# A two-block transformer kernel on one core: state copies on ScalarE, states advanced one direction per level, the output gate's product a chunk earlier, output projection from level 0 of the last chunk

## The reference, cut to what matters

```python
pc = hc @ w_in[:, :COL_Q]                       # 256 context tokens: keys, values, decays
s_f = gla_final_state(kc, vc, gfc)              # the states that the recurrence starts from
s_b = gla_final_state(flip(kc), flip(vc), flip(gbc))

def step(s, inp):                               # gla_chunked: a chunk of tokens
    b = jnp.cumsum(gc, axis=1)
    o_inter = einsum('bihk,bhkv->bihv', qc * exp(b), s)
    att = einsum('bihk,bjhk,bijhk->bijh', qc, kc, exp(b_i - b_j) masked)
    o_intra = einsum('bijh,bjhv->bihv', att, vc)
    s_new = s * exp(b_last) + einsum('bjhk,bjhv->bhkv', kc * exp(b_last - b), vc)

o_gla = rmsnorm(o_f + o_b, g_head) * silu(og)   # og: 512 columns of x @ w_in
o_sc = sb * dwconv_row(sc * sx, w_sc, b_sc)     # sb, sc, sx: columns of x @ w_in
yx = concatenate([o_gla, o_sc])
x = x + gt1 * rmsnorm(yx @ w_out, g_post_mix)
```

## Time and profile before

| | us |
|---|---|
| median of three runs | 1448.08 (1447.05 to 1450.49) |
| the profiled execution | 1445.49 |
| its span, first to last instruction | 1443.7 |
| around the span | 1.8 |
| granted TensorE clock, mean | 0.978 |

### The profile page before, as it was taken

The page is one execution under the profiler, slowest core; times in us unless marked ns, Lnnn a source line. Parts: engine busy times, 40 slices in busy tenths (PEclk is TensorE's granted clock), DMA queues, the critical chain, the costliest instruction groups (busy, mean ns, idle before and its releaser), DMA issues.

```text
span 1443.7 us, 19719 instructions
## 1 busy us (share of the span) xinstructions
PE 1378.6 (95%) x6923; PEld 1113.7 (77%) x6923; DVE 895.8 (62%) x1274; ACT 397.4 (28%) x757; POOL 836.0 (58%) x651
## 2 busy tenths in 40 slices
PE   6899899998799999999999999999899999999998
PEld 4678678877488888887877888676688888888887
DVE  4687687753766666673028699646766888886000
ACT  3442223322422222201013202355413333332000
POOL 1343434426566666677756677532367777777775
PEclk8999999989799999999989999999999999999999
DMA  9457222112033333354332333221133333333332
GB/s 355 150 186 221 57 57 60 59 45 84 16 94 98 102 89 100 98 156 140 102 88 73 89 88 88 73 59 44 42 91 88 102 93 96 102 89 94 92 94 84
DMA packets 224459, 142.05 MB, mean 98 GB/s; under 512 B 5611, under 2 KB 211088, under 8 KB 224400
## 3 DMA queue, kind: packets, MB, share of 16 engines
q1 hardware_dynamic: 221333, 136.45, 31.6%
q10 hardware_dynamic: 3067, 4.78, 1.0%
HBM read 139.12 MB, written 2.10 MB: 98 GB/s over the span
## 4 chain that ended last, share of the span: by engine, by line
PE 83%; DVE 9%; issue 3%; POOL 2%; ACT 2%; DMA 0%; POOLq 0%; SPq 0%; DVEq 0%; ACTq 0%
PE ps L555 25%; PE ps L557 24%; PE ps L556 24%; PE ps L853 2%; DVE norm_acc L1713 1%; POOL w_lo L518 1%; DVE ada_acc L1810 1%; PE ps L1096 1%; PE ps L1125 1%; PE ps L1112 1%; DVE SS L2015 1%; ACT h_hi L1210 1%; DVE xT L2186 1%; POOL w_hi L515 1%; DVE h_lo L1734 1%
## 5 line engine op out<-in xcount | busy, mean ns | idle before, releaser
L518 POOL TENSOR_TENSOR w_lo<-raw,w_hi 128x1024 fp32r<-128x1024 f32 x213 | 535.5, 2514 | 17.8
L555 PE MATMUL ps<-h_hi,w_hi 128*128 128x512 f32 x1064 | 426.2, 401 | 13.2 <-DVE h_lo L1734 8.3
L557 PE MATMUL ps<-h_hi,w_lo 128*128 128x512 f32 x1064 | 417.5, 392 | 0.0
L556 PE MATMUL ps<-h_lo,w_hi 128*128 128x512 f32 x1064 | 417.4, 392 | 0.0
L514 POOL TENSOR_TENSOR w_hi<-raw,cst 128x16 fp32r<-128x16 f32 x213 | 62.3, 292 | 560.3 <-PE ps L557 503.7
L555 PEld LDWEIGHTS ps<-h_hi,w_hi 128*128 128x128 f32 x1064 | 201.5, 189 | 66.4 <-issue 18.3
L557 PEld LDWEIGHTS ps<-h_hi,w_lo 128*128 128x128 f32 x1064 | 201.5, 189 | 43.6
L556 PEld LDWEIGHTS ps<-h_lo,w_hi 128*128 128x128 f32 x1064 | 202.0, 190 | 39.6
L515 POOL TENSOR_SCALAR w_hi<-raw 128x1008 fp32r<-128x1008 f32 x213 | 232.4, 1091 | 0.0
L2104 DVE SCALAR_TENSOR_TENSOR f_acc<-ps,par,f_acc 128x441 f32<-128x441 f32 (+2 forms) x176 | 122.3, 695 | 50.2 <-ACT f_acc L1210 27.9
L555 PE MATMUL ps<-f_hi,w_hi 128*128 128x512 f32 x352 | 138.3, 393 | 0.6 <-POOL w_lo L518 0.6
(11 more groups left out here) (301 smaller groups left out, 1958.0 us busy)
## 6 DMA issues: line engine op xcount, KB each, us to landing
raw<-in_w_up SPq DMA_DIRECT2D x88, 512.0 KB, 3.7
raw<-in_w_in SPq DMA_DIRECT2D x59, 512.0 KB, 3.7
raw<-in_w_down SPq DMA_DIRECT2D x32, 512.0 KB, 3.7
ada_first<-in_w_ada SPq DMA_DIRECT2D x8, 1024.0 KB, 10.2
raw<-in_w_out SPq DMA_DIRECT2D x16, 512.0 KB, 3.5
v_tok<-in_w_ada SPq DMA_DIRECT2D x14, 512.0 KB, 5.3
raw<-in_w_down SPq DMA_DIRECT2D x16, 384.0 KB, 3.3
ada<-in_w_ada SPq DMA_DIRECT2D x10, 512.0 KB, 4.9
```

What stands on the lines that cost most here:

```text
L518: pool.tensor_tensor(w_lo[:, slot % 2, :], raw[:, slot, :], w_hi[:, slot % 2, :].bitcast(F32), ALU.subtract).then_inc(S("lo_split"), 1)
L555: nc.tensor.matmul(dst, lhs_hi, rhs_hi, start=first, stop=False)
L556: nc.tensor.matmul(dst, lhs_hi, rhs_lo, start=False, stop=False)
L557: return nc.tensor.matmul(dst, lhs_lo, rhs_hi, start=False, stop=last)
```

## The change

Five edits, all in the mixer of the first block.

1. `keep_state` moves from VectorE to ScalarE. ScalarE's row n of the key loop is now `key_decay(n)`, `keep_state(n-1)`, the copy of the turned keys n. The exp of `dec` into `small` (what the states are multiplied with) is made at n = 2, not at n = 5.
2. The states advance one direction at a time, 4 instructions each: `forward(0)` to `forward(2)` in the key loop (n = 3 to 5), `backward(0)` ahead of chunk 0, `forward(3)` in level 1, `backward(1)` to `backward(3)` in levels 2 to 4.
3. The output gate: the tanh of og moves from level 0 of its own chunk to level 4 of the chunk before (`branch_tanh`), its product from level 0 to level 5 of the chunk before (`branch_gate`); for chunk 0 they stand in the key loop and ahead of chunk 0. Bank 0 is thus free a chunk earlier, and the semaphores of the branch are counted anew.
4. `out_s` is given out by the table `MIX_EARLY`: in levels 0, 1 and 2 of chunk 3 the first three k of tiles 0, 1, 2 (9 matmuls each), in level 3 their last k (9), in levels 4 and 5 half of tile 3 each (6), in level 6 tile 4 (12). The last k needs the branch half of chunk 3 (`ys`), which is made in level 2. `MIX_BANKS` is reordered, so that a tile's bank is one that is free by then.
5. `head_gate` is made chunk by chunk, in levels 2, 4 and 5 of chunk 3.

```diff
-    MIX_BANKS = [0, 1, 2, 3, 7, 4, 5, 6]
+    MIX_BANKS = [0, 2, 3, 1, 7, 4, 5, 6]
...
+        MIX_EARLY = [[(0, 0, 3)], [(1, 0, 3)], [(2, 0, 3)], [(0, 3, 4), (1, 3, 4), (2, 3, 4)], [(3, 0, 2)], [(3, 2, 4)], [(4, 0, 4)]]
+        def mix_early(n):
+            free = {0: ("gated_og", CHUNKS), 1: ("branch_act", 2 * CHUNKS), 2: ("branch_dve", 2 * CHUNKS - 1), 3: ("branch_dve", 2 * CHUNKS)}
+            for m, k0, k1 in MIX_EARLY[n]:
+                if k0 == 0 and m in free:
+                    pe.wait_ge(S(free[m][0]), free[m][1])
+                out_tile("out_s", m, ys_hi, ys_lo, 0, range(k0, k1))
...
-                elif n >= 2:
-                    if n == 2:
-                        pe.wait_ge(S("branch_act"), 2 * CHUNKS)
-                        pe.wait_ge(S("branch_dve"), 3 * CHUNKS)
-                    out_tile("out_s", n - 2, ys_hi, ys_lo, 0)
+                else:
+                    mix_early(n)
...
+        def keep_state(n, c):
+            act.wait_ge(S("state_mm"), n + 1)
...
+            for dst, src in todo:
+                ins = activate(dst, src, ACT.Copy)
+            ins.then_inc(S("state_read"), 1)
...
+            if n >= 1:
+                keep_state(n - 1, STATE_ORDER[n - 1])
             act.wait_ge(S("ke_turned"), n + 1)
...
             activate((g_qe, g_att)[n % 2][:, :], ps[:, 4 + 3 * (n % 2), :], ACT.Copy).then_inc(S("ket_copied"), 1)
+            if n == 3:
+                branch_tanh(0)
...
+        act.wait_ge(S("ket_copied"), ALL_CHUNKS)
         exp_level(0)
+        keep_state(ALL_CHUNKS - 1, STATE_ORDER[-1])
...
+                elif n == 4 and c < CHUNKS - 1:
+                    branch_tanh(c + 1)
...
+        def forward(n):
+            dve.wait_ge(S("decay_ready"), 1)
+            dve.wait_ge(S("state_read"), n + 2)
...
-            if n >= 1:
-                keep_state(n - 1, STATE_ORDER[n - 1])
-        keep_state(ALL_CHUNKS - 1, STATE_ORDER[-1])
+            if n >= 3:
+                forward(n - 3)
...
         offset(0)
         offset(1)
+        branch_gate(0)
+        backward(0)
+        dve.wait_ge(S("ke_turned"), ALL_CHUNKS)
         decayed(0)
...
-                if c == 0 and 2 <= n < 2 + CHUNKS:
-                    if n > 2:
-                        dve.wait_ge(S("states_done"), n - 2)
-                    advance_states(n - 2)
-                if n == 5 and c == CHUNKS - 1:
-                    head_gate(False)
+                if c == 0 and n == 1:
+                    forward(CHUNKS - 1)
+                elif c == 0 and 2 <= n < 1 + CHUNKS:
+                    backward(n - 1)
+                if n == 5 and c < CHUNKS - 1:
+                    branch_gate(c + 1)
+                if c == CHUNKS - 1 and n in (2, 4, 5):
+                    head_gate((0, 1, 2)[(2, 4, 5).index(n)])
```

More of the change, by code:

```diff
@@ L797, in branch @@
                 if tile >= 1:
-                    pe.wait_ge(S("branch_act" if n == 2 else "branch_dve"), (3 * tile, 3 * tile, 2 * tile, 3 * tile - 2)[n] - (n == 0))
+                    done = (("gated_og", tile), ("branch_dve", 2 * tile), ("branch_act", 2 * tile), ("branch_dve", 2 * tile - 1))[n]
+                    pe.wait_ge(S(done[0]), done[1])
                 elif n == 0:
@@ L887, in head_spread, with out_tile @@
             mm.then_inc(S("o_spread"), 1)
-        def out_tile(name, m, hi, lo, ready):
+        def out_tile(name, m, hi, lo, ready, ks=range(4)):
             u = FIRST[name] + m // 2
             first = name == "out_s"
-            if m % 2 == 0:
+            if m % 2 == 0 and ks[0] == 0:
                 wait_unit(u)
-            for k in range(4):
+            for k in ks:
                 if m == 0:
@@ L901, in out_tile @@
                             hi[:, k, :], lo[:, k, :], first and k == 0, not first and k == 3)
+            if ks[-1] < 3:
+                return
             if m % 2:
@@ L1349, in _, with branch_tanh @@
         act.wait_ge(S("gate_done"), 2)
+        def branch_tanh(i):
+            act.wait_ge(S("units_done"), FIRST["branch"] + 4 * i + 1)
+            activate(og[:, i, :], ps[:, 0, :], ACT.Tanh, scale=0.5).then_inc(S("branch_act"), 1)
         def key_decay(n):
@@ L1395, in branch_in @@
         def branch_in(i):
[L1397 to L1400, removed]
+            act.wait_ge(S("units_done"), FIRST["branch"] + 4 * i + 3)
             if i >= 1:
-                act.wait_ge(S("branch_dve"), 3 * i)
+                act.wait_ge(S("branch_dve"), 2 * i)
             if i >= 2:
@@ L1407, in branch_center @@
         def branch_center(i):
-            act.wait_ge(S("branch_dve"), 3 * i + 1)
+            act.wait_ge(S("branch_dve"), 2 * i + 1)
             if i >= 1:
@@ L1873, in ke, with advance, backward @@
             ins.then_inc(S("ke_ready"), 1)
[L1875 to L1883, removed]
+        def advance(rows, dst, src, c):
+            for h in range(GH):
+                cols = slice(h * P, (h + 1) * P)
+                ins = vec.scalar_tensor_tensor(dst[rows, cols], src[rows, cols],
+                                               small[rows, h * ALL_CHUNKS + c:h * ALL_CHUNKS + c + 1],
+                                               dst[rows, cols], ALU.mult, ALU.add)
+            return ins
+        def forward(n):
+            dve.wait_ge(S("decay_ready"), 1)
+            dve.wait_ge(S("state_read"), n + 2)
+            if n:
+                dve.wait_ge(S("forward_done"), n)
+            src, c = (SS[:, n - 1, :], n - 1) if n else (s_tmp, CHUNKS + 1)
+            advance(slice(0, DK), SS[:, n, :], src, c).then_inc(S("forward_done"), 1)
+        def backward(n):
+            m = CHUNKS - 1 - n
+            dve.wait_ge(S("state_read"), ALL_CHUNKS if n else 2)
+            if n:
+                dve.wait_ge(S("backward_done"), n)
+            src, c = (SS[:, m + 1, :], m + 1) if n else (s_tmp, CHUNKS)
+            advance(slice(DK, P), SS[:, m, :], src, c).then_inc(S("backward_done"), 1)
         for n in range(10, EARLY_KEYS):
@@ L1996, in head_scale, with head_gate @@
                 .then_inc(S("head_scaled"), 1)
[L1998 to L2002 removed]
+        def head_gate(c):
+            tok = slice(c * P, (c + 1) * P)
+            dve.wait_ge(S("head_scaled"), c + 1)
+            dve.wait_ge(S("gated_og"), CHUNKS)
             vec.tensor_tensor(oT[:, :, tok], oT[:, :, tok], og[:, :, tok], ALU.mult).then_inc(S("head_gated"), 1)
[L2005 removed]
+        dve.wait_ge(S("ke_ready"), ALL_CHUNKS)
         offset(0)
         offset(1)
+        branch_gate(0)
+        backward(0)
+        dve.wait_ge(S("ke_turned"), ALL_CHUNKS)
         decayed(0)
[L2009 to L2025 removed]
         dve.wait_ge(S("masks_loaded"), 16)
@@ L2056, in _ @@
         head_scale(CHUNKS - 1)
-        head_gate(True)
+        head_gate(CHUNKS - 1)
         for h in range(GH):
```

37 lines of the change are left out of this document (12 added, 25 removed).

## The result

In the comparison made for the prediction the changed kernel took 1440.16 us (median, 1437.6 to 1442.81, 6 runs) and the kernel before 1448.6 us (1445.69 to 1450.49, 6 runs): ratio 0.9947, 95% interval 0.993 to 0.9963. The profiled execution of the changed kernel took 1442.81 us (span 1441.0). A second comparison, with more runs, gave 1441.9 us (10 runs) against 1445.75 (28 runs): ratio 0.9967, interval 0.9953 to 0.998. The two intervals have only gains of some 5 to 7 us in common. The forecast was 1439; its sum was 9.3 us. The trace shows that one of the two terms of this sum was right and the other wasn't.

What follows compares the result with a forecast made beforehand. PE was busy 95% of the span, so only its waits and lower clock could be won. 3.5 us (chunk 0 with key loop) plus 5.8 (chunk 3) made 9.3 off 1448.08: 1439 us, range 1433.5 to 1444.

Steps and rivals of the forecast that it cites:

- Chunk 3: Last chunk: early out tiles bring `outputs` at 313.5 us against 319.36, 5.8 us gained, bounds 3.4 and 9.1.
- rival B: PE is fed nearly throughout: 7 of 8.3 us in chunk 0, 8 of 9.1 in chunk 3; 1434, chance 0.15.
- Key loop: Chain from a states product to the next turn of keys, with ScalarE's copies: 0.6 us lost, bounds 0 and 1.4.
- ScalarE's copies "back to back": In the key loop, copies of 0.594 us each were taken 0.5 apart, making a turn's chain 3.5 us.
- Chunk 0: VectorE sets the pace; 4.6 us less state work, 1.0 taken back by GpSimd hold-ups, bounds -1.5 and +3.5.
- rival A: VectorE keeps the pace: 1.0 gained in chunk 0 with key loop, 3.4 to 4 in chunk 3; 1443, chance 0.2.
- The clock: PE's clock sank after idles of 2.3 and 1.6 us; idles up to 1.1 in the key loop left it 1.00.
- PE still isn't the limit: In chunk 0, PE's own levels would end at 200 us, against 203.4 for VectorE after the change.
- Behind the mixer: Tail after chunk 3's output: every distance stays that of before.
- C: Key loop: PE idles some 2 us a turn, the clock falls to 1.2 GHz; 4 slower, 1452, chance 0.04.
- D: Early tiles or chunk 1's branch wait for unit or bank as before; 0 to 2 us gained, 1447, chance 0.06.
- signs of being wrong: Key loop over 1.5 us longer, states above 0.5, chunk 3's level 3 not 12.6 behind level 0, chunk 0 above 39.

Runs made afterwards that it cites:

- the hoisted kernel: Changed kernel with the key decay of n + 1 put ahead of the state copy on ScalarE: 1437.39 us, ratio 0.9935 to the kernel before.
- the one with pieces for 20 units: Changed kernel with the key decay hoisted and `w_lo` made in four instructions for units 8 to 27: 1431.42 us, ratio 0.99 to the kernel before.

## Why the prediction was right and wrong, step by step

**Chunk 3: right.** Predicted 5.8 us, measured 5.9. Level 1 came 3.5 us behind level 0 with no idle time in place of 2.3, level 3 at 301.32, 12.6 behind level 0 as predicted, PE idle for 0.59 and 0.76 us before levels 3 and 4, at a clock of 1.00. The kernel without this edit takes 32.4 us for the distance, so 5.6 of the 5.9 us go with this edit. One sum of the prediction is off here: chunk 3's own work isn't 23.6 us. Chunks 1 and 2, always fed, take 33.1 to their output with 96 matmuls of projections; with 60 at the same 0.23 us each that leaves 24.9. So 7.8 us were lost before and not 9.1, and rival B's 8 of them weren't to be had.

**Key loop: two terms were too small, ScalarE's copies "back to back" at 0.5 apart and what GpSimd holds up.** Predicted 0.6 us lost, bounds 0 and 1.4, measured 1.6. ScalarE and VectorE of one turn of the changed kernel:

```profile
153.93 0.59 ACT L1221 ACTIVATE SS<-ps 64x512 f32<-64x512 f32 x1 [2.95 <-PE ps L827]
154.53 0.59 ACT L1221 ACTIVATE s_tmp<-ps 64x512 f32<-64x512 f32 x1
155.15 0.60 ACT L1221 ACTIVATE g_qe<-ps 128x512 f32<-128x512 f32 x1
155.65 0.62 ACT L1221 ACTIVATE g_e<-g_e 128x512 f32<-128x512 f32 x1
```

```profile
157.00 0.69 DVE L1903 TENSOR_TENSOR g_z<-g_e,p 64x512 f32<-64x512 f32 x1
...
159.44 2.88 DVE L1891 TENSOR_TENSOR g_e<-B,dec 128x512 f32<-128x512 f32 x1
```

The two state copies and the copy behind them start 0.60 and 0.62 us apart, no quicker than one takes alone; the exp starts 0.5 behind its copy. In the turn with one state copy all four start 0.48 to 0.49 apart. From the start of the first copy to the next turn of keys it is 3.8 us, not 3.5, in three turns. In the fourth it is 4.4: `ke_offset` (the row of 159.44) takes 2.88 us and not 0.69 beside a `w_lo` that runs from 158.67 to 161.78, and PE waits 1.63 us; with `w_lo` left out it waits 0.83. There the prediction expected 0.3 us of gain. Worse, the chain was taken as given, while one line's move takes the key decay out of it, as the hoisted kernel shows.

**Chunk 0: the work was sized right, the hold-ups by GpSimd wrong.** Predicted: 4.6 us less work, 1.0 of it lost to more hold-ups (time for which an instruction of VectorE takes longer than alone), bounds -1.5 and +3.5. Measured without `w_lo`: 4.0 us less. Measured with it: from c_p to the end of `take` 5 the hold-ups, added up from the rows, went from 3.2 us (1.5, 0.3 and 1.4) to 7.0 (1.7, 0.3, 2.0 and 2.9), 3.7 more and beyond the bound. VectorE's row became 0.9 us shorter (30.1 in place of 31.0), and even that didn't reach the output. VectorE, then GpSimd, in chunk 0 of the changed kernel:

```profile
179.04 2.38 DVE L1970 TENSOR_TENSOR g_e<-B 128x512 f32<-128x512 f32 x1
...
184.17 1.13 DVE L1910 SCALAR_TENSOR_TENSOR SS<-SS,small 64x128 f32<-64x128 f32 x4
...
188.34 3.16 DVE L1910 SCALAR_TENSOR_TENSOR SS<-SS,small 64x128 f32<-64x128 f32 x4
...
198.27 4.08 DVE L1910 SCALAR_TENSOR_TENSOR SS<-SS,small 64x128 f32<-64x128 f32 x4
...
206.43 1.30 DVE L1997 COPY_PREDICATED g_att<-masks,ps 128x256 f32<-128x256 int32 x2
```

```profile
178.48 2.40 POOL L518 TENSOR_TENSOR w_lo<-raw,w_hi 128x1024 fp32r<-128x1024 f32 x1
...
187.85 2.68 POOL L518 TENSOR_TENSOR w_lo<-raw,w_hi 128x1024 fp32r<-128x1024 f32 x1
...
198.15 1.03 POOL L515 TENSOR_SCALAR w_hi<-raw 128x1008 fp32r<-128x1008 f32 x1
199.26 2.39 POOL L518 TENSOR_TENSOR w_lo<-raw,w_hi 128x1024 fp32r<-128x1024 f32 x1
```

Four state instructions take 1.13 to 1.16 us alone, 3.16 beside the `w_lo` of 187.85, and 4.08 beside `w_hi` of 198.15 and `w_lo` of 199.26 both. In the group that starts at 198.27 the first instruction takes 1.05 us, while `w_hi` ends at 199.18, and the second 2.57, while `w_lo` ends at 199.26 + 2.39 = 201.65; the group ends at 202.35. I had counted a hold-up as one instruction of 2.4 us met once per unit. A row of short instructions with SBUF operands that was under way while `w_hi` ran was caught by both, 1.03 + 2.39 us, here and twice in the kernel with only the gate and the out tiles. Before the change only one row of states in four was caught, by one of them. The chance of the forecast should have lain nearer to rival A, which had this mechanism and the place; but A still expected 1.0 us gained from chunk 0 and the key loop together, and 1.5 to 1.8 were lost.

**The clock: my reading of idle time was too kind, and "PE still isn't the limit" failed by it.** I wrote that it sank after idles of 2.3 and 1.6 us and stood up to 1.1. PE alone, stretches of 2 us (length, busy, granted clock, DMA) of the changed kernel:

```profile
188.00:190.00 2.00, 2.00 (x16) 0.75 0.00 0
190.00:192.00 2.00, 2.00 (x6) 0.50 0.18 20
...
206.00:208.00 2.00, 2.00 (x6) 0.51 0.00 0
```

After idles of 1.23 and 1.21 us the clock was 0.75 and then 0.50, and after 1.15 us 0.51, while 1.63 us in the key loop left it at 1.00. That made part of chunk 0's loss. `take` 5 ends at 206.43 + 1.30 = 207.7 us, but level 6, which began just behind it before the change, starts at 210.24. PE isn't idle between level 5 at 204.67 and level 6; it takes 5.6 us for what takes 4.0 at full clock, so 1.6 us are the clock's. The 28.25 of 33 us busy contain these matmuls at 1.2 GHz. With `w_lo` left out the clock stays at 1.00.

**Behind the mixer: not foreseen.** I said every distance there would be as before. In both profiles of the changed kernel the clock falls during the spread behind the out tiles (L632) and not after it, which costs 1.0 us up to the first f_act. This needn't be the change: the kernel before with `w_lo` in pieces has the same 1.0 us (the spread takes 2.08 us there), while the kernel with only the gate and the out tiles (1.16), the hoisted one (1.22) and the one with pieces for 20 units (1.16) don't. Why the clock falls there earlier isn't settled.

**The total.** The stretch gained about 3.3 us, not 9.3; the medians of the first comparison differ by 8.4, those of the second by 3.9. The kernel before took 1448.6 us in the first and 1445.8 to 1447.1 in the three later comparisons, and between two executions of the changed kernel 3.0 us come and go behind the first f_act. So forecast and first measurement agree by luck: the sum was 6 us too much, and six runs each showed some 5 us more than the stretch gives. Not all of that is shown to be chance. The stretch's 3.3 us lie inside the second interval and outside the first, and the rows of four profiles can't tell whether the edits also shift something behind the first f_act. Rivals C and D didn't occur: the clock stood in the key loop, and no early tile waited for its unit or bank. What the prediction gave as signs of being wrong came in two places: the key loop was longer by 1.6 us (above 1.5), and chunk 0 stayed at 39.9 to its output.

## What to carry to other kernels

Before moving short VectorE instructions whose operands all lie in SBUF, lay them over GpSimd's row: a move that halves such work can cost as much as it saves, and it did so in both profiled executions alike. When an operation is moved to another engine, write down the whole chain that it joins, and ask which link could run ahead of the wait. For a gain of under 1%, read the stretch between two instructions in two profiles beside the medians, and say so where the two differ.

## What the runs showed of the hardware that I had not expected

- From the first turn of keys to the end of chunk 3, 170 us, VectorE's starts in two executions of the changed kernel agree within 0.05 us, and the distance itself differs by 0.4 us in two of the kernel before. In the second block the two of the changed kernel part by steps of 1.6 and 1.5 us.
- An instruction with SBUF operands on VectorE waits for the end of GpSimd's, and a row of four was caught twice: 4.08 us for 1.16 us of work. Beside one whole `w_lo` such a row took 3.16 us, beside one cut in four 2.95.
- The granted clock halved after idles of 1.2 us in chunk 0 and did not after 1.63 us in the key loop; the idle time alone doesn't decide it. How long it stays down differs as well: after the same wait for og it was 0.50 up to 181 us in one kernel and up to 182 in another whose wait had begun 1.5 us earlier.
